# Stage boundaries of a two-block float32 kernel: order of splits, sums, layer norms and matmul pairs

## The reference

```python
# first block
h  = x + rmsnorm(concat(ssd(...), pool(...)) @ w_out, g1)          # mixer, input rmsnorm(x) @ w_in
h  = h + rmsnorm((gelu(conv3(gate)) * val) @ w_down, g2)          # gate, val = rmsnorm(h) @ w_up
h  = h + rmsnorm(sigmoid(rmsnorm(h) @ w_ple_gate) * (p @ w_ple), g3)
# second block, ALPHA = 4 ** 0.25
h  = layer_norm(ALPHA * h + fox(h) @ fox_w_out, ln_g[0], ln_b[0])  # gated attention, 16 heads
h  = layer_norm(ALPHA * h + ret(h) @ ret_w_out, ln_g[1], ln_b[1])  # retention, 8 heads
```

## Time and profile before

| | us |
|---|---|
| median of 3 runs | 2510.44 (2508.97 to 2512.79) |
| profiled execution, its time | 2511.03 |
| its span | 2509.2 |
| PE busy in the span | 2429.5 (97%) |
| PEld busy | 2100.3 |
| DVE busy | 1705.9 |
| ACT busy | 1249.8 |
| POOL busy | 598.3 |

### The profile page before, as it was taken

The page is one execution under the profiler, slowest core; times in us unless marked ns, Lnnn a source line. Parts: engine busy times, 40 slices in busy tenths (PEclk is TensorE's granted clock), DMA queues, the critical chain, the costliest instruction groups (busy, mean ns, idle before and its releaser), DMA issues.

```text
span 2509.2 us, 34416 instructions
## 1 busy us (share of the span) xinstructions
PE 2429.5 (97%) x13596; PEld 2100.3 (84%) x13596; DVE 1705.9 (68%) x2276; ACT 1249.8 (50%) x1752; POOL 598.3 (24%) x580
## 2 busy tenths in 40 slices
PE   7999989999999999989999999997999999999996
PEld 6877878888888888888788888886888888888886
DVE  7897577775566765477666766768666675666676
ACT  5766454444344444465555555634444453444444
POOL 4163163221012221252200000026221210221234
PEclk9999999999999999999999999998999999999998
DMA  6444646665566665555455555563555656565662
GB/s 239 132 139 149 226 144 189 190 187 185 185 196 190 188 189 178 179 174 175 133 165 175 149 171 168 151 185 121 171 179 184 188 177 196 163 187 177 188 182 88
DMA packets 126674, 434.93 MB, mean 173 GB/s; under 512 B 13488, under 2 KB 21040, under 8 KB 126512
## 3 DMA queue, kind: packets, MB, share of 16 engines
q1 hardware_dynamic: 126512, 432.72, 55.8%
HBM read 430.57 MB, written 2.10 MB: 172 GB/s over the span
## 4 chain that ended last, share of the span: by engine, by line
PE 88%; DVE 5%; POOL 3%; ACT 3%; issue 1%; DMA 0%; SPq 0%; ACTq 0%; POOLq 0%; DVEq 0%
PE bank L566 87%; POOL acc L1751 2%; DVE wlo L1215 1%; DVE S L1218 1%; POOL hT L1751 1%; ACT whi L853 1%; DVE xa L1218 1%; DMA raw<-in_w 0%; ACT S L889 0%; DVE S L1215 0%; PE bank L778 0%; DVE ev L1218 0%; DVE ev L1224 0%; ACT L1048 0%; ACT L1097 0%
## 5 line engine op out<-in xcount | busy, mean ns | idle before, releaser
L1215 DVE TENSOR_TENSOR wlo<-raw,whi 128x1024 fp32r<-128x1024 f32 (+1 forms) x822 | 1030.3, 1261 | 684.6 <-ACT whi L853 682.6
L853 ACT ACTIVATE whi<-raw 128x1024 fp32r<-128x1024 f32 (+1 forms) x822 | 847.4, 1040 | 809.8 <-PE bank L566 805.6
L566 PE MATMUL bank<-xa,whi 128*128 128x512 f32 (+1 forms) x3968 | 1131.0, 397 | 18.9 <-DVE wlo L1215 12.2
L566 PEld LDWEIGHTS bank<-xa,whi 128*128 128x128 f32 x3968 | 663.0, 189 | 95.0 <-DVE wlo L1215 15.0
L566 PEld LDWEIGHTS bank<-xa,wlo 128*128 128x128 f32 x3936 | 638.0, 189 | 107.8
L566 PE MATMUL bank<-xa,wlo 128*128 128x256 f32 x3936 | 665.6, 281 | 0.0
L566 PE MATMUL bank<-xb,whi 128*128 128x512 f32 (+1 forms) x1948 | 513.3, 376 | 1.1 <-ACT S L1022 1.1
L566 PEld LDWEIGHTS bank<-xb,whi 128*128 128x128 f32 x1948 | 324.0, 190 | 31.8 <-DVE wlo L1215 1.3
L566 PEld LDWEIGHTS bank<-xb,wlo 128*128 128x128 f32 x1776 | 289.2, 190 | 40.5
L566 PE MATMUL bank<-xb,wlo 128*128 128x256 f32 x1776 | 314.3, 281 | 0.0
L566 PE MATMUL bank<-whi,xa 128*128 128x512 f32 x768 | 244.5, 400 | 16.6 <-DVE wlo L1215 7.3
(11 more groups left out here) (190 smaller groups left out, 1412.8 us busy)
## 6 DMA issues: line engine op xcount, KB each, us to landing
raw<-in_w SPq DMA_DIRECT2D x792, 512.0 KB, 3.8
raw<-in_w SPq DMA_DIRECT2D x29, 256.0 KB, 2.7
hT<-in_xT SPq DMA_DIRECT2D x4, 512.0 KB, 7.7
hT<-in_xT SPq DMA_DIRECT2D x1, 2048.0 KB, 11.3
out<-hT SPq DMA_DIRECT2D x4, 512.0 KB, 3.0
X<-in_dec SPq DMA_DIRECT2D x8, 192.0 KB, 3.8
con<-in_con SPq DMA_DIRECT2D x1, 768.0 KB, 12.0
hT<-in_rcnt SPq DMA_DIRECT2D x1, 512.0 KB, 4.2
```

The source lines that it names most:

```text
L566: return pe.matmul(o, w, x, start=start, stop=stop, skip_group_check=True)
L853: act.activation(hi, r, ACT.Copy).then_inc(*w_high(i))
L1215: return dve.tensor_tensor(o, x, y, op)
```

## The change

- `AT_ONCE` goes: for each k tile of a turned block, `whi` for j = 0 and 1, then `wlo` for j = 0 and 1.
- The first of the five taps goes from DVE to ACT. `dt_turn` is placed one piece later, `cums` two pieces later, the heads at 19/4 pieces for two of them instead of 5, beginning one piece later.
- `h_factor` for r = 0 and 1 goes from 9 to 12 pieces into the stage. The first two blocks of these stages are done in turn, piece by piece (`side_by_side`); the steps behind them move accordingly.
- `res` steps for r = 0 and 2 are spread over 4 pieces. `res_rows` takes `acc` first. The low halves of tiles 0 and 1 are made earlier.
- Layer norms: tiles 10 to 13 are summed on PE earlier; the square of the mean goes to DVE; ACT asks for a square root ahead of time; the mean is subtracted by POOL for 4 tiles and by DVE for 12, most of it two tiles at a time; DVE multiplies by the reciprocal without the gain, and ACT applies gain and bias into `hT`; the high half is a copy of `hT`; `h_again` goes. In the first norm the splits of two pieces are held back and done within the norm.

```diff
-AT_ONCE = {"w_in": 4, "w_out": 4, "w_ffn_up": 1, "w_ffn_down": 2, "w_ple": 1, "w_ple_gate": 1, "fox_w_in": 2,
-           "fox_w_out": 4, "ret_w_in": 4, "ret_w_out": 1, "pool0": 1, "pool1": 1, "pool2": 1, "pool3": 1}
...
+    def side_by_side(*blocks):
+        pair = [begin(kind, arg, operand) for kind, arg, operand, _, _ in blocks]
+        for k in full:
+            for b, (_, _, _, mat, col) in zip(pair, blocks):
+                u = use(b, mat, col, *k, first=k == full[0], last=k == full[-1])
+        return [u - 1, u]
...
-        late(u + 9, "h_factor", r)
+        late(u + (9 if r < 0 else 12), "h_factor", r)
...
-            late(e + 1, "dt_turn")
-            late(e + 3, "cums")
+            late(e + 2, "dt_turn")
+            late(e + 5, "cums")
             for h in range(16):
-                t = e + 6 + 5 * (h // 2) + 2 * (h % 2)
+                t = e + 7 + 19 * (h // 2) // 4 + 2 * (h % 2)
...
     for j in range(0, 16, 2):
-        place(ends["mix"], 4, ("res", 0, j))
+        place(ends["mix"] + j // 4, 4, ("res", 0, j))
...
-            d = 7 if f == 0 else 2
+            d = {0: 7, 2: 3}.get(f, 2)
...
-            d = 5 if f == 0 else 1
+            d = {0: 8, 2: 2}.get(f, 1)
...
-        d = {0: 7, 2: 3}.get(c, 1)
+        d = {0: 7, 2: 6, 4: 3}.get(c, 1)
...
     for j in range(0, 16, 2):
-        place(e, 4, ("res", 2, j))
+        place(e + j // 4, 4, ("res", 2, j))
...
+        late(n + 25, "early_mean", layer, EARLY)
+        late(n + 30, "early_mean", layer, EARLY + 2)
...
-    place(ends["fox_out"], 4, ("h_again",))
...
+        HELD = (ends["fox_out"] - 1, ends["fox_out"])
+        BY_POOL = 4
+        GROUPS = ((0, 1), (1, 2), (2, 4), (4, 6), (6, 8), (8, 10), (10, 12), (12, 14), (14, 16))
...
# scalar_program and vector_program
-                if 0 <= u < N - AHEAD:
+                if 0 <= u < N - AHEAD and u not in HELD:
                     split(u + AHEAD)
...
# scalar_program
+                    elif step == "conv_taps" and k[1] == 0:
+                        c, _, _ = k
+                        for j in range(2):
...
+                            act.activation(conv_y(c, j), conv_pad(c, j)[:, 0:T], ACT.Identity, scale=pc("conv_w", 5 * (c + j)),
+                                           bias=pc("conv_b", c + j)).then_inc(*act_val("tap", c, j))
...
+                                if i == KT - 3:
+                                    act.activation(spare, eps5, ACT.Sqrt)
...
-                        act.activation(acc[:, :], rs[:, :], ACT.Square).then_inc(*act_val("mean_squared", l))
...
+                        if l == 0:
+                            split(HELD[0] + AHEAD)
+                        for j in range(KT + 1):
+                            if j < KT:
+                                q.wait_ge(*vec_val.of("normed", l, j))
+                                act.activation(hT[:, j, :], S2[:, j, :], ACT.Identity, scale=pc("ln_g", 16 * l + j),
+                                               bias=pc("ln_b", 16 * l + j)).then_inc(*act_val("h_normed", l, j))
+                            if j and l == 0:
...
+                                act.activation(xa[:, j - 1, 0:T], hT[:, j - 1, :], ACT.Copy).then_inc(*x_high("xa", 4, j - 1))
+                                if j == 7:
+                                    split(HELD[1] + AHEAD)
...
# vector_program
+                            if j in (1, 2):
+                                operand_low(r, j - 1)
...
+                        tt(rs2[:, :], rs[:, :], rs[:, :], ALU.mult).then_inc(*vec_val("mean_squared", l))
...
+                        for i, (first, last) in enumerate(GROUPS):
+                            root, mean = (r[:, :].unsqueeze(1).broadcast_to((128, last - first, T)) for r in (rs2, rs))
+                            if first < BY_POOL:
+                                q.wait_ge(*pool_val.of("cent", l, last - 1))
+                            else:
+                                tt(S2[:, first:last, :], S2[:, first:last, :], mean,
+                                   ALU.subtract).then_inc(*vec_val("cent", l, first))
+                                q.wait_ge(*vec_val.now())
+                            tt(S2[:, first:last, :], S2[:, first:last, :], root,
+                               ALU.mult).then_inc(*vec_val.both(*[("normed", l, j) for j in range(first, last)]))
+                            if l == 0 and i:
+                                operand_lows(*GROUPS[i - 1])
+                                if i in (4, 7):
+                                    split(HELD[i // 7] + AHEAD)
```

More of the change, by code:

```diff
@@ L203, in layout @@
             f = 22 * half + 2 * q
-            e = block("gate", f, ("xa", 1), "w_ffn_up", 128 * f, full)
-            d = 7 if f == 0 else 2
+            v = None
+            if f == 0:
+                e, v = side_by_side(("gate", 0, ("xa", 1), "w_ffn_up", 0), ("val", 0, ("xa", 1), "w_ffn_up", FF))
+            else:
+                e = block("gate", f, ("xa", 1), "w_ffn_up", 128 * f, full)
+            d = {0: 7, 2: 3}.get(f, 2)
             late(e + d, "gate_scale", f)
@@ L229, in layout @@
     for c in range(0, 16, 2):
-        e = block("pgate", c, ("xa", 2), "w_ple_gate", 128 * c, full, "half" if c == 14 else "turned")
-        d = {0: 7, 2: 3}.get(c, 1)
+        if c == 0:
+            first_two = side_by_side(*[("pgate", i, ("xa", 2), "w_ple_gate", 128 * i) for i in (0, 2)])
+        e = first_two[c // 2] if c < 4 else block("pgate", c, ("xa", 2), "w_ple_gate", 128 * c, full,
+                                                   "half" if c == 14 else "turned")
+        d = {0: 7, 2: 6, 4: 3}.get(c, 1)
         late(e + d, "pgate_scale", c)
@@ L574, in piece @@
                 q.wait_ge(*w_low.of(u))
[L575 to L594, removed]
-                                    m.then_inc(*piece_tile.both(("tile", n), *([("used", u)] if j == b.tiles - 1 else [])))
-                                elif k == s.n - 1 and j == b.tiles - 1:
-                                    m.then_inc(*piece_tile("used", u))
-                    return
                 for k in range(s.n):
@@ L617, in piece @@
                             m = mm(B[:, 0:T], lo_[:, k, c], x[:, 0:T], False, stop)
+                        else:
+                            c = slice(128 * j, min(128 * j + 128, s.cols))
+                            mm(B[0:c.stop - c.start, :], hi[:, k, c], x, start)
+                            continue
+                        if k == s.n - 1 and s.last:
+                            m.then_inc(*piece_tile.both(("tile", n), *([("used", u)] if j == b.tiles - 1 else [])))
+                        elif k == s.n - 1 and j == b.tiles - 1:
+                            m.then_inc(*piece_tile("used", u))
+                    for j in range(b.tiles if b.form == "turned" else 0):
+                        n, c = b.tile + j, slice(128 * j, min(128 * j + 128, s.cols))
+                        m = mm(bank[n % 4][0:c.stop - c.start, 0:T], lo_[:, k, c], x[:, 0:T], False, s.last and k == s.n - 1)
                         if k == s.n - 1 and s.last:
@@ L705, in tensor_program @@
                         for t in range(2):
-                            c = slice(128 * t, 128 * t + 128)
-                            mm(bank[4][:, t:t + 1], acc[:, c], ones[:, 0:1], True)
-                            for i in range(2):
-                                q.wait_ge(*squares.of("sum", r, 14 + i))
-                                m = mm(bank[4][:, t:t + 1], sq[:, i, c], ones[:, 0:1], False, i == 1)
+                            mm(bank[4][:, t:t + 1], acc[:, 128 * t:128 * t + 128], ones[:, 0:1], t == 0)
+                        for i in range(2):
+                            q.wait_ge(*squares.of("sum", r, 14 + i))
+                            for t in range(2):
+                                m = mm(bank[4][:, t:t + 1], sq[:, i, 128 * t:128 * t + 128], ones[:, 0:1], False, i == 1)
                         m.then_inc(*side("res_sums", r))
@@ L1887, in pool_program @@
                         q.wait_ge(*act_evac.of("mean", l))
-                        for j in range(KT):
+                        for j in range(BY_POOL):
                             tt(S2[:, j, :], S2[:, j, :], rs[:, :], ALU.subtract).then_inc(*pool_val("cent", l, j))
-                    elif step == "h_again":
-                        for j in range(KT):
-                            q.wait_ge(*x_high.of("xa", 4, j))
-                            pool.tensor_scalar(hT[:, j, :], S2[:, j, :], pc("ln_b", j), None,
-                                               ALU.add).then_inc(*pool_val("h_again", j))
                     elif step in ("rq", "rk"):
```

97 lines of the change are left out of this document (45 added, 52 removed).

## The result

The changed kernel takes 2493.38 us (median of 4 runs, 2492.48 to 2494.23), the kernel before 2510.5 beside it (4 runs): a ratio of 0.993, 95% interval 0.9916 to 0.9944. It is faster by 17.1 us, not by 31: inside the range, and the size of the rival "half kept". The profiled execution took 2493.88 us, its span is 2492.0 (before 2509.2).

A forecast was written before the change was run, and what follows sets the result against it. PE, busy 97% of the span, bounds the kernel, so only its stops, half-clock time and matmul work count; terms of 5.5, 2.5, 2.4, 5.9, 2.4, 5.5, 2.0 and 4.9 sum to 31.1 us, forecasting 2479.5, range 2468 to 2497.

The forecast's parts named there:

- half kept: Rival, chance 0.20: stops that go uncover others at the `dt` turn and first norm; about half, 15 us, remains: 2495.
- `dt` turn: Mixer: PE's 3.69 us wait for DVE's bank copy and the slow clock behind it go; 5.5 us saved, bounds 3 to 6.4.
- with `cums` two pieces later PE should just miss waiting: Mixer, behind the `dt` turn: DVE's chain of small operations ends about where it was, so no new PE wait.
- Last head: Mixer's end: PE's 2.62 us wait for DVE's last head weights goes, moved one piece up; 2.5 saved, bounds 0 to 3.
- r = 0: Feed-forward start: POOL wait and clock, 5.6 us, go, less most of a new wait; 2.4 saved, bounds 0 to 5.6.
- a wait for L1224, near 357, of 3.4: Feed-forward start: new PE wait of 3.4 us for DVE's copy of `gate 0` from its bank, behind three more splits.
- r = 1: Gate start: POOL stop of 3.89 and 1.7 of clock go, plus 0.3 for reordered `res_rows`; 5.9 us in the sum.
- r = 2: Attention start: earlier low half and splits between `res` steps put the eighth piece at 1225.8, not 1228.2; 2.4 saved.
- First layer norm: Earlier reciprocal and shorter DVE work bring piece 570's `wlo` 4.3 us sooner, plus 1.2 of clock; 5.5 saved, bounds 3 to 9.
- a first wait for ACT of 1.2: First layer norm: DVE's only counted wait for ACT, 1.2 us, within 20.7 from the reciprocal to piece 570's `wlo`.
- Last layer norm: Kernel's end: DVE's stretch of 11.32 us becomes 9.7, with 0.3 from the mean's square; 2.0 saved, bounds 1 to 3.
- Pair order: All matrices in the first order: 240 pieces at 0.0055 and 178 at 0.020 us (`w_ffn_down`, `fox_w_in`); 4.9 saved.

The follow-up runs named there:

- run 8: Changed kernel with the squares of the first gate block (r = 0) three pieces later: 2489.87 us, ratio 0.9916.
- run 5: Changed kernel with the first two transposes of x (tiles 0 and 1) one piece later: 2492.67 us, ratio 0.9926.
- run 4: Changed kernel with `dt_turn` and `cums` back behind the pieces they stood behind before, heads kept: 2494.21 us, ratio 0.9925.
- run 6: Changed kernel with the first two x transposes, and the last two taps and silu of convolution tile 0, one piece later: 2490.71 us, ratio 0.9918.
- run 7: run 2's kernel with the split that fills piece 570 also held for the middle of the first layer norm: 2485.57 us, ratio 0.9898.
- run 10: Changed kernel with the `res` steps of r = 0 and r = 2 together again behind their stage's last piece: 2493.02 us, ratio 0.9925.
- run 9: Changed kernel with `h_factor` back at 9 pieces into the stage for r = 0 and 1: 2499.76 us, ratio 0.9952.
- run 3: Changed kernel with gate 0 and val 0 one after the other again at the feed-forward start: 2495.61 us, ratio 0.9929.
- run 2: Changed kernel with DVE's low halves in the first layer norm one more group of tiles later: 2487.84 us, ratio 0.9898.
- run 1: Kernel before with only the pair order changed, every `AT_ONCE` entry 1: 2507.2 us, ratio 0.9983.
- run 12: Changed kernel with the edits of run 5, run 7 (including run 2's) and run 8 together, and `h_factor` of r = 0 one piece later: 2478.1 us, ratio 0.9864.

## Why the prediction was half right

- **`dt` turn, 5.5 predicted, 1.4 measured.** The 3.69 went as forecast. The step that failed is "with `cums` two pieces later PE should just miss waiting": it waits 0.82. And a wait was overlooked altogether: `cums` moved onto the piece where the first transpose of x stands, which needs ACT's copy of the sums first. It cost 1.47 us, 2.04 where PE came to it at full clock (run 8), and went in run 5. These two with the clock (1.8, run 8 against the changed kernel at piece 27) are 4.1, the whole gap at piece 27, where 1.4 are saved.
- **Last head, 2.5 and 2.3.** Right in size, in part by luck: the head weights' wait of 2.62 went, and 1.8 came back at once, as POOL's sum for the gate's norm made PE wait 2.91 in place of 1.12. The sum has only the first. That the table still shows 2.3 comes of its line at piece 60: the last head's matmuls, 1.08 us, now stand ahead of that piece, and so count against the row above and for this one, which would be about 1 without them. (Another 1.2 were saved between pieces 27 and 59; their source was not looked for.)
- **r = 0, 2.4 and 0.3.** The mechanism was foreseen: a wait for L1224, near 357, of 3.4; it stands at 356.30 with 2.31. The step that failed is the price: the clock fell behind the new wait (0.60 over 356.3 to 360.5), which the sum had counted as saved, and the first pieces lost another microsecond. Where the clock held behind the same wait (runs 4, 6 and 7), this part saves 2.4, 1.8 and 2.4: the forecast's 2.4 fits the executions without a new fall of the clock, and has no term for the others. Run 8 shows that POOL's squares between the adds made the copy late, as the prediction had it; run 10 that the spread did.
- **r = 1, 5.9 and 5.9.** Right, and run 9 loses 6.7 there.
- **r = 2, 2.4 and 1.1.** The stop of 1.23 went and the first tile came 0.67 sooner (PE's idle at the start 1.99, was 2.66), together the 1.9; the sum's further 0.5 isn't there, and PE ran at half clock for 10.2 us where it had been 6.8. Runs 3 and 5, with the same code and 6.8 there, save 2.2 and 1.9.
- **First layer norm, 5.5 and 0.4.** The reciprocal came 3.2 us earlier against piece 560 (3.55 predicted), the wide operation takes 0.70 (0.68 predicted). What failed is the term "a first wait for ACT of 1.2": the wait is in every group, 1.13, 0.97, six of 0.64, 0.38 and 0.49, 6.8 us together. From the reciprocal's end to piece 570's `wlo` it is 25.9 us (1707.04 to 1732.9) in place of 20.7. Run 2 takes most of these waits away, and the part is 6.0 us shorter. The sum also had PE's stops shorter, with 1.2 us of clock won: they went from 6.6 and 6.12 to 5.35 and 6.31, and both still have half a clock behind them.
- **Last layer norm, 2.0 and 2.1.** DVE's stretch is 9.34 us (9.7 predicted).
- **Pair order, 4.9 and 3.6 (4.0 in run 1).** In `w_ffn_down` 82 pieces gave 1.64, 0.020 each, as taken. In `fox_w_in` 96 pieces gave 1.2 and not 1.9: the price of `w_ffn_down` was carried over to a matrix of which no row was read.
- **The chances.** 17.1 of 31.1 us were kept; the time lies in the range, but the rival that came was "half kept", and for its reason: each stop that goes uncovers another. The forecast held against it that the stops stem from order, with the engine idle later. That is so, but the order that the change makes has stops of its own, and they were not looked for piece by piece at the `dt` turn and in the norm, as they were at r = 0. Runs 2 and 7 get 6.0 and 2.5 us in the norm by moving work, with no less of it, and run 8 up to 3.4 at r = 0. Run 12 stands at 2478.1, where the forecast was: the time was there to be had, in this design, with five further moves.

## What to carry to other kernels

When a producer and a consumer are on two engines that each go through their steps in program order (DVE makes, ACT rounds, DVE subtracts), write out one full period of both before a stretch is priced: a lag of one group that cost 0.64 us cost it in six groups here, and with a lag of two only the waits at the two ends were left (0.53, 0.37 and 0.49 in run 2). When a step is moved, list what already stands at its new place and what that waits for. And where a stop goes, count its clock as saved only once the next stop is known to be absent, and then as a range: behind the same new wait of 2.3 us the clock fell in some profiles and held in others.

## What the runs showed that was not expected

- **The granted clock differs between executions of the same code.** The changed kernel and runs 2, 3, 7, 8, 9 and 10 have the same instructions up to the feed-forward part. At 74 to 80 us the changed kernel had clock 0.50 and run 8 1.00, each behind the same wait of 0.82 at `cums`. (The wait at the transpose comes later, and is the shorter for the fall, 1.47 against 2.04 us, as PE gets to it later.) In three of the seven (the changed kernel, run 2, and for half as long run 7) it fell there, in four it did not; where it fell, the pieces behind it end 1.5 to 1.8 us later. In runs 3 and 7 it fell at 236 to 245 us, at the wait of 2.9 for POOL's sum, and cost 2.7 to 2.8; in the other five it held. At the bank copy of r = 0 six kernels have the same code and a wait of 2.30 to 2.32; it fell in the changed kernel and runs 2 and 5, and held in runs 4, 6 and 7. The changed kernel's window behind that wait, then run 4's:

```profile
356.30:360.50 4.20, 4.16 (x13) 3.36 (x14) 4.20 (x5) 0.75 (x1) 3.77 (x4) 0.60 0.85 300
```

```profile
358.40:362.60 4.20, 4.16 (x22) 3.40 (x23) 4.20 (x5) 1.53 (x2) 3.77 (x4) 1.00 0.88 297
```

A single profile cannot price such a stretch, and a gain of 2 us is not shown by one.
- **The same matmuls cost more in another order.** 0.020 us for a piece of 16 matmuls in `w_ffn_down`, at full clock and with no wait, when two k tiles are taken together; 0.013 in `fox_w_in` (1.2 us over 96 pieces). Why the two differ was not tried.
- **Pairing tiles saves DVE little.** The operation of 512 columns takes 0.70 us (1.41 for two), that of 256 takes 0.38 (0.76 for two, at 1707.07). What shortened the last norm in spite of DVE's new subtractions is read from the trace of before, first norm: the multiplication takes 0.96 us while POOL subtracts beside it, up to 1731.55 (1730.87 in the earlier trace rows), and 0.47 from then on (POOL is then on `h_again`):

```profile
1732.37 0.47 DVE L1218 SCALAR_TENSOR_TENSOR S<-S,par,rs 128x256 f32<-128x256 f32 x1
```

After the change POOL's subtractions end at 2477.41, before DVE's stretch begins at 2477.66. The smaller operation (no gain in it, 0.38) can have done little more; no run takes the two apart.
